# Two recurrence units per weight tile, and five Winograd pairs of gate tiles in place of three

## What is computed

```python
z = xn @ w_in
q, k, v, o, ig, fg, u, vb, ga, gb = split_in(z)
h, C, n, m = mlstm_branch(q, k, v, ig, lf, C, n, m)
y_a = (sigmoid(o) * h) @ w_a
y_b = spatial_gate(gelu(u), vn, w_s, b_s) @ w_b
x = x + (sigmoid(ga) * y_a + sigmoid(gb) * y_b) @ w_o
```

```python
# one chunk of one head
num = einsum('nhts,nhsv->nhtv', s, v) + w_inter[..., None] * einsum('nhvk,nhtk->nhtv', C, q)
h = num / maximum(abs(den), exp(-m_t))[..., None]
C_new = decay[..., None, None] * C + einsum('nhs,nhsv,nhsk->nhvk', w_last, v, k)
```

## Time and profile before

| what | us |
|---|---|
| median of 3 runs | 900.88 (900.83 to 901.25) |
| the profiled execution's own time | 900.66 |
| its span, first to last instruction | 898.8 |
| PE busy | 890.2 (99%) |
| DVE busy | 595.8 (66%) |
| ACT busy | 386.0 (43%) |
| POOL busy | 134.9 (15%) |
| mean granted TensorE clock | 0.998 |

### The profile page before, as it was taken

The page is one execution under the profiler, slowest core; times in us unless marked ns, Lnnn a source line. Parts: engine busy times, 40 slices in busy tenths (PEclk is TensorE's granted clock), DMA queues, the critical chain, the costliest instruction groups (busy, mean ns, idle before and its releaser), DMA issues.

```text
span 898.8 us, 19220 instructions
## 1 busy us (share of the span) xinstructions
PE 890.2 (99%) x7330; PEld 885.9 (99%) x7330; DVE 595.8 (66%) x946; ACT 386.0 (43%) x613; POOL 134.9 (15%) x182
## 2 busy tenths in 40 slices
PE   8999999999999999999999999999999999999997
PEld 8999999999999999999999999999999999999997
DVE  7895774443884445677755677777777778966544
ACT  7545434534863323344433344444444444433334
POOL 0673000002541111000005800000000000000001
PEclk9999999999999999999999999999999999999999
DMA  6332253234872222322355222222222222333232
GB/s 213 114 123 94 71 205 101 72 102 156 285 277 77 72 70 70 97 90 94 96 179 137 91 93 93 93 93 93 86 84 89 92 93 88 98 107 87 90 106 96
DMA packets 31495, 100.37 MB, mean 112 GB/s; under 512 B 4668, under 2 KB 7260, under 8 KB 31192
## 3 DMA queue, kind: packets, MB, share of 16 engines
q1 hardware_dynamic: 29256, 92.96, 31.5%
q0 software_dynamic: 1472, 5.72, 2.1%
q10 hardware_dynamic: 720, 1.04, 0.4%
HBM read 92.37 MB, written 7.35 MB: 111 GB/s over the span
## 4 chain that ended last, share of the span: by engine, by line
PE 91%; POOLq 3%; issue 3%; DMA 1%; POOL 1%; ACT 0%; SPq 0%; ACTq 0%
PE out L1924 84%; PE trp L1924 3%; PE aux L1924 2%; POOLq L1902 2%; POOLq L1900 1%; PE trp L1956 1%; DMA cwb<-in_conv_wb 1%; DMA raw_pair<-in_w_slots 1%; PE aux L2113 0%; POOL y L1915 0%; POOL out_conv_old L1886 0%; ACT xg L579 0%; POOLq L1893 0%; POOLq L87 0%; POOL sconv L1894 0%
## 5 line engine op out<-in xcount | busy, mean ns | idle before, releaser
L579 ACT ACTIVATE whi<-raw_pair 128x1024 fp32r<-128x1024 f32 (+3 forms) x164 | 154.5, 947 | 227.4 <-PE out L1924 213.6
L1068 DVE TENSOR_TENSOR wlo<-raw_pair,whi 128x1024 fp32r<-128x1024 f32 (+1 forms) x127 | 162.6, 1280 | 131.0 <-ACT whi L579 130.6
L1924 PE MATMUL out<-xh,whi 128*128 128x260 f32 x708 | 149.5, 288 | 0.0
L1924 PE MATMUL out<-xh,wlo 128*128 128x260 f32 x708 | 145.5, 283 | 0.0
L1924 PE MATMUL out<-xl,whi 128*128 128x260 f32 x708 | 145.4, 283 | 0.0
L1924 PE MATMUL out<-x2h,wlo 128*128 128x260 f32 x704 | 142.0, 283 | 0.0
L1924 PE MATMUL out<-x2h,whi 128*128 128x260 f32 x704 | 141.9, 283 | 0.0
L1924 PE MATMUL out<-x2l,whi 128*128 128x260 f32 x704 | 141.7, 283 | 0.0
L1924 PEld LDWEIGHTS out<-xh,whi 128*128 128x128 f32 x708 | 110.8, 189 | 0.5
L1924 PEld LDWEIGHTS out<-xh,wlo 128*128 128x128 f32 x708 | 110.3, 188 | 0.0
L1924 PEld LDWEIGHTS out<-xl,whi 128*128 128x128 f32 x708 | 110.2, 188 | 0.0
(11 more groups left out here) (362 smaller groups left out, 1683.0 us busy)
## 6 DMA issues: line engine op xcount, KB each, us to landing
raw_pair<-in_w_slots SPq DMA_DIRECT2D x123, 512.0 KB, 3.3
raw_pair<-in_w_dn SPq DMA_DIRECT2D x16, 448.0 KB, 3.3
c_ring<-in_C_state SPq DMA_DIRECT2D x8, 512.0 KB, 5.5
row<-scratch SPq DMA_DIRECT2D x8, 512.0 KB, 6.1
out_C_sample<-c_ring SPq DMA_DIRECT2D x8, 512.0 KB, 5.0
raw_pair<-in_w_dn SPq DMA_DIRECT2D x8, 512.0 KB, 3.5
xres<-in_x_all POOLq DMA_DIRECT2D x1, 1560.0 KB, 6.7
x<-in_x_all SPq DMA_DIRECT2D x5, 260.0 KB, 6.7
```

What stands on the lines that cost most here:

```text
L579: return act.activation(out, in_, func, **kw_)
L1068: TT(wlo[p][:, 0:width], raw[p][:, 0:width], whi[p][:, 0:width].bitcast(F32), ALU.subtract)\
L1924: return pe.matmul(*a, **k)
```

## The change

`WHOLE = NC + 2 = 6` BY pairs of tiles are plain, and five blocks follow: the first is of gate b (tiles 6 and 7, with the branch tiles of b), the other four of gate a (tiles 0 to 7). There are no plain AY steps any more. The number of slots and their order in memory stay.

The 16 units ride in the first 8 BY tiles, two in each: the products of unit 2m behind k-tile 0 and of unit 2m+1 behind k-tile 4; the transposes of unit 2m-1 behind k-tile 2 and of unit 2m behind k-tile 6. Tile 8 has the transposes of unit 15 behind k-tile 2. The loops over chunks are written out. All sums and differences of x now stand behind the last unit, beside BY tiles 8 to 11.

```diff
-PLAIN = 2
+WHOLE = NC + 2
 DOWN_PAIRS = 3
+GATE_PAIRS = KT - WHOLE // 2
...
-                self.n = [At(S_AY + 2 * PLAIN + 4 * q + t) for t in range(4)]
+                self.n = [At(S_BY + 2 * WHOLE + 4 * q + t) for t in range(4)]
+                self.of_b = q == 0
                 self.t0, self.t1 = self.n[0].c % 2, self.n[1].c % 2
-                self.j = PLAIN + 2 * q
+                self.j = WHOLE if self.of_b else 2 * q - 2
...
+            for m in range(2 * NC):
+                if m >= 1:
+                    split(At(S_BY + m + 1))
+                if m % 2 == 1:
+                    if m == 1:
+                        act.wait_ge(s_hal, 1)
+                    gate_sigmoid(At(S_BY + m - 1), m // 2 % 2)
+                unit_scaled(2 * m)
+                if m >= 1:
+                    unit_hi(2 * m - 1)
+                unit_scaled(2 * m + 1)
+                unit_hi(2 * m)
...
+            for m in range(2 * NC):
+                unit_denominator(2 * m)
+                if m >= 1:
+                    unit_gated(2 * m - 1)
+                    low(At(S_BY + m + 1))
+                if m % 2 == 0 and m >= 2:
+                    if m == 2:
+                        for r in range(4):
+                            dve.wait_ge(s_cs[r], 32)
+                    first_branch(At(S_BY + m - 1), m // 2 - 1, (m // 2 - 1) % 2)
+                if m >= 1:
+                    unit_low(2 * m - 1)
+                unit_denominator(2 * m + 1)
+                unit_gated(2 * m)
+                unit_low(2 * m)
...
+            def by_plain(i):
+                n = At(S_BY + 1 + 2 * i)
+                last = i == WHOLE - 1
+                if i == NC:
+                    unit_gated(NC * NH - 1)
+                    low(n)
+                    x_sum(0, 0, 0)
+                    first_branch(n.plus(-2), i - 1, (i - 1) % 2)
+                    unit_low(NC * NH - 1)
+                    x_sum(1, 0, 1)
+                    dve.drain()
+                    x_difference(0, 1, 0)
+                    x_sum(2, KT // 2, 1)
+                    dve.drain()
+                    x_difference(1, 2, 1)
+                    x_difference(2, 2, 0)
+                    low(n.plus(1))
+                    x_combination_low(0, 1)
                     x_sum(3, KT // 2, 0)
                     dve.drain()
                     x_difference(3, 3, 2)
-                    x_combination_low(2, 1)
+                    x_combination_low(2, 2)
                 if last:
                     x_combination_low(1, 3)
                     factor_low(pairs_w[0], 0)
                     factor_low(pairs_w[0], 1)
                     weight_sums(pairs_w[0])
...
+                first_branch(n, i, i % 2)
...
             def unit_transposes(c, t):
                 b = At(B_UNIT + t, c, 4)
+                pe.wait_ge(s_p, c * NH + t + 1)
...
+            def by_tile(m):
+
+                u = 2 * m
+                c, t = u // NH, u % NH
+                mids = {0: lambda: unit_products(c, t, c == 0), 4: lambda: unit_products(c, t + 1, c == 0),
+                        6: lambda: unit_transposes(c, t)}
+                if m >= 1:
+                    mids[2] = lambda: unit_transposes((u - 1) // NH, (u - 1) % NH)
+                tile(At(S_BY + m), *((xh, xl) if m % 2 == 0 else (hbh, hbl)), mids=mids)
```

More of the change, by code:

```diff
@@ L311, in hybrid_layer @@
         pairs_d = [DownPair(i) for i in range(DOWN_PAIRS)]
-        pairs_w = [Pair(q) for q in range((KT - PLAIN) // 2)]
+        pairs_w = [Pair(q) for q in range(GATE_PAIRS)]
         def vb_slot(j):
@@ L805, in _, with unit_scaled, unit_hi, gate_sigmoid @@
             A(hah[:, :, SEQ:TOK], so[:, :, SEQ:TOK]).then_inc(s_hah, 1)
[L808 to L823, removed]
+            def unit_scaled(u):
+                t = u % 2
+                act.wait_ge(s_rd, u + 1)
+                A(hn[t][:, :], trp[t][:, 0:2, :].rearrange("p a b -> p (a b)"), scale=nd[:, t, 2:3]).then_inc(tre[t], 1)
+            def unit_hi(u):
+                c, t = u // NH, u % NH
+                act.wait_ge(s_p, u + 2)
+                A(hah[:, 2 * t:2 * t + 2, c * P:(c + 1) * P], so[:, 2 * t:2 * t + 2, c * P:(c + 1) * P]).then_inc(s_hah, 1)
+            def gate_sigmoid(n, g):
+                ready(n)
+                A(both(ftmp[g][:, :]), out2(n), ACT.Sigmoid).then_inc(evac[n.c % 2], 1)
+            for m in range(2 * NC):
[10 more added lines that the diff above has]
+                unit_hi(2 * m)
             def merged_hi(j):
@@ L863, in ay_plain @@
                     split(n.plus(2))
[L864 to L866 removed]
+                gate_sigmoid(n, i % 2)
+                if i == NC:
+                    x_combination_hi(2)
                     x_combination_hi(1)
                 if last:
+                    x_combination_hi(3)
                     next_factors_hi(pairs_w[0])
@@ L907, in ay_pair @@
                     next_factors_hi(pairs_w[q + 1])
-                merged_hi(pr.j + 1)
-            for i in range(PLAIN):
-                ay_plain(i)
+                if not pr.of_b:
+                    merged_hi(pr.j + 1)
+            for i in range(NC, WHOLE):
+                by_plain(i)
             for pr in pairs_w:
@@ L1409, in unit_step @@
                 dve.reciprocal(nd[:, b, 2:3], nd[:, b, 1:2]).then_inc(s_rd, 1)
-                dve.wait_ge(s_unit, c * 4 + (t + 1))
+                dve.wait_ge(s_unit, u + 1)
                 STT(state[:, t, :], state[:, t, :], decay[:, c, t:t + 1], aux[:, 0, 0:DVA], ALU.mult, ALU.add)\
                     .then_inc(s_st, 1)
[L1413 to L1417, removed]
@@ new lines, in unit_low, with first_branch @@
+            def unit_low(u):
+                dve.wait_ge(s_hah, u + 2)
+                part = unit_part(u)
+                TT(hal[part], so[part], hah[part].bitcast(F32), ALU.subtract).then_inc(s_hal, 1)
+            def first_branch(n, j, g):
+                ready(n)
+                evacuated(dve, n.plus(-1))
+                TT(both(merged[:, j, :]), both(ftmp[g][:, :]), out2(n), ALU.mult).then_inc(evac[n.c % 2], 1)
+            for m in range(2 * NC):
[13 more added lines that the diff above has]
+                unit_low(2 * m)
@@ L1554, in ay_pair @@
                     first_gate_sum(pairs_w[q + 1])
-                merged_low(pr.j + 1)
-            for i in range(PLAIN):
-                ay_plain(i)
+                if not pr.of_b:
+                    merged_low(pr.j + 1)
+            for i in range(NC, WHOLE):
+                by_plain(i)
             for pr in pairs_w:
@@ L1924, in MM, with tile @@
                 return pe.matmul(*a, **k)
-            def tile(n, hi, lo, k0=0, nk=KT, bank=None, use=None, start=True, stop=True, mid=None, mid_at=3, each=None, end=None):
+            def tile(n, hi, lo, k0=0, nk=KT, bank=None, use=None, start=True, stop=True, mid=None, mid_at=3, each=None, end=None, mids=None):
                 p = n.c % 2
@@ L1943, in tile @@
                         mid()
+                    if mids is not None and k in mids:
+                        mids[k]()
                 m.then_inc(done, 1)
```

117 lines of the change are left out of this document (46 added, 71 removed).

## The result

| what | before | after |
|---|---|---|
| median, us (15 runs each) | 900.83 (900.57 to 901.53) | 902.76 (902.38 to 905.48) |
| the profiled execution's own time | 900.66 | 902.47 |
| its span | 898.8 | 900.1 |

The ratio is 1.0023, with a 95% interval of 1.0016 to 1.0030: slower by 1.93 us by the medians. The forecast was 902.8, with 1.9 us more.

The account below looks back on a forecast made before the run. The prediction took PE, busy 890.2 of 898.8 us, as the bound: waits of 2.0 + 0.1 + 1.9 + 0.9 = 4.9 us, less 2.99 for matmuls, give 1.9 us more, 902.8 us; range 900.5 to 904.9.

Parts of the forecast that it names:

- The matmuls: Two more gate pairs become blocks: 24 matmuls less on PE, 2.88 us, with 0.11 us of an old wait 2.99 less.
- The recurrence's steady state: BY tiles with two units: about 8.8 us each, DVE's 5.3 us of work fits, no wait, cost zero.
- The first BY tile: Unit 1's products behind k-tile 4 wait for unit 0's state update on DVE: 2.0 us, bounds 1.6 to 2.4.
- Behind the last unit: BY tiles 8 to 11: PE waits for DVE's queue, 0.1 us for a bank, 1.9 at tile 10, 0.9 at 11.
- T+2.65: T is the start of BY tile 8; DVE can start unit 15's gated product 2.65 us after it.
- T+13.64: The end of slot 10's low part on DVE, 13.64 us after the start of BY tile 8.
- The weights of the first block: Loaded into the buffer slot 11 frees, landing 3.3 us after issue; summed in time, half a microsecond to spare.
- the three signs: Signs of being wrong: second wait under 1 us, two-unit tile over 9 us, block of gate b waiting for weights.
- The drain rule: Full durations for DVE's operations, 0.07 us more each, would make the three waits about 3.5 us; the prediction used start spacings.
- rival 4: PE's clock falls to 1.2 GHz for one tile behind a wait: 5.8 us more, 908.6 us; chance 0.03.
- rival 1: The combinations hide in DVE's queue in BY tiles 8 and 9: 2.9 us of waits vanish, 899.9 us; chance 0.10.
- rival 2: Only the first BY tile's wait of 2.0 us is missing: 900.8 us; chance 0.09.

Follow-up runs that it names:

- e9: e5 with DVE's operations beside BY tiles 8 to 11 reordered so that none stands in front of ACT's result; 898.24 us.
- e6: The changed kernel with two more DVE additions of 128x1040, result unused, in each of five two-unit tiles; 902.64 us.
- e1: The changed kernel with unit 0's denominator and state update on DVE moved ahead of the last operations on the sample rows; 901.30 us.
- e2: The changed kernel with unit 1's products in the first BY tile moved from behind k-tile 4 to behind k-tile 7; 901.72 us.
- e11: The changed kernel with GpSimd's last product of the sample rows held until VectorE's updates of the step before are over; 905.37 us.
- e5: e4 with two sums of x moved into two of the recurrence's two-unit tiles; 899.02 us.
- e7: The changed kernel with one more DVE addition of 128x1040, result unused, ahead of the low part of slot 10; 903.91 us.
- e4: The changed kernel with the edits of e1 and e3 together; 899.16 us.
- e8: The changed kernel with four blocks, all of gate a, and eight plain BY pairs; 903.41 us.
- e3: The changed kernel with low parts of slots 10 and 11 ahead of differences and combinations' low parts, two of the latter moved into the block; 900.79 us.

## Why the prediction was right

**The matmuls.** Right. 24 are gone, and e9, without waits, has a stretch 3.08 us shorter than before (2.99 computed).

**The recurrence's steady state at zero.** Right, and safer than I had it. The first eight BY tiles take 69.79 us (263.34 to 333.13), 1.47 of them the wait, with no other gap, and BY tiles 2 to 7 last 8.74 to 8.79 us, where 8.8 was forecast. e6 shows 2.3 us of room per tile where I had argued with 0.7.

**The first BY tile, 2.0 us.** Right in mechanism (e1, e2, e11), too large by 0.5: 1.47. The step that failed is "nothing ahead of it on DVE has changed", which took 268.77 for a fixed start. The denominator began at 268.06. Of the 0.7 us, 0.59 is the group of eight updates: 3.29 us in the profiled execution of before, 2.70 in that of after, by the meeting with POOL. That is a difference of two executions, not of the two kernels: in e5 the same group took 3.79. The rest of the chain was as computed: the state update ended at 269.13, PE went on 0.14 later.

**Behind the last unit, 0.1 + 1.9 + 0.9.** Measured 0.06, 1.62 and 0.64. DVE's queue was computed well: T+2.65 was T+2.55, T+13.64 was T+13.43. The mis-sized term is the step from a low part's end to the tile that waited, 0.14 us from rows 9; here it is 0.05, twice. Each wait costs a little more than its gap, since the first matmuls behind it are slower: tile 10, whose first two take 0.51 us instead of 0.40, lasts 5.88 us without the gap at its end (346.61 to 353.13, less 0.64), where a plain tile lasts 5.76.

**The weights of the first block, "met, with half a microsecond to spare".** Wrong, and one of the three signs that the prediction itself named. The load was issued at 353.10 and the sums began at 357.71, 4.6 us later; I had taken the median of 3.3 us over the whole kernel (and 20.3 + 3.3 + 2.8 is 26.4, not 26.6). The block took 10.44 us, 0.36 more than the 10.08 of the others, where I had allowed none. This load took 4.3 to 4.7 us in each of the six kernels with this order, and the block 10.57 us in e1, 10.14 in e2, 10.21 in e6, 10.58 in e7 and 10.54 in e11. In the traces of e4 and e9, whose low parts come early, no such wait is seen.

**The drain rule.** DVE's starts were 1.13 to 1.15 us apart for operations of 1.22 to 1.24 (345.34, 346.48, 347.63; 351.86, 352.99, 354.14). With full durations the prediction had the waits 0.6 us longer, and they were shorter than forecast. The Trainium skill (VectorE: DVE Perf Modes, The DRAIN you can't avoid) says that the next operation does not start until the pipeline is empty, but the same section adds that an operation that is not held starts earlier, which the prediction left out. This trace agrees with the addition, for operations that do not read each other's result.

**The clock.** Waits of 1.3 and 1.5 us left the granted clock at 1.00 in both stages, the 2.4 GHz level, and matmuls at 0.12 us: rival 4 did not occur. It is 1.00 behind the longer waits of e7 (2.62 us) and e11 (2.76 us) too.

**The sum.** By e9, all waits cost 4.44 us instead of 4.9. So the stretch grew by 1.36 us, not 1.9. The profiled execution's own time grew by 1.81 and the median by 1.93. The rest lies in no stage: the span without the stretch is 696.1 us before and after (898.8 - 202.69 and 900.1 - 204.05). What grew is the time of an execution beyond its span, from the first to the last instruction: 1.9 us in the profiled execution of before, 2.4 in that of after. It is 1.80 to 1.91 us in each of 78 executions of the kernel before, 1.78 to 2.47 in those of the changed kernel (median 2.12), much the same in the other kernels with five blocks, and 1.81 to 1.90 in e8 with four. So it is not a chance of single executions. It goes with what e8 takes back, the fifth block, which is of gate b; why it does stays open. The two errors, 0.5 too much of waiting and some 0.5 of which no step spoke, cancelled: that the forecast was met to 0.04 us is luck; that PE waits for DVE at the three named places, and roughly how long, is not.

**Rivals 1 and 2.** They were a matter of order and not of capacity. e3 is rival 1 made by hand (899.9 forecast, 900.79 measured), and e1 is rival 2 (900.8 and 901.30); e9 is their common case, forecast as 897.9 and measured as 898.24.

## What to carry to other kernels

When work is taken off the bound engine and the helper engine's work is pushed together to make room, the average load does not say whether it fits. Add up the helper's queue by the spacing of its starts between the two events that fix it, and compare with the moment at which the bound engine needs each result. Operations that nobody awaits soon belong in front of a wait that exists anyway. Ahead of the low part for the next tile they may stand only as long as its input is not there: in e5 that low part stood first and DVE idled for 2.26 us, in e9 a sum and a difference fill this time, while in the changed kernel six of them made PE wait. e9 does the same work as the changed kernel in another order and is 4.5 us faster. A start time read from one execution is a sample; look for a releaser in brackets that is a DMA ahead of it, and keep its effect in the range.

## What the hardware showed unexpectedly

VectorE (DVE) and GpSimd (POOL) block each other. A VectorE update with two operands in SBUF (0.34 us alone) that started beside a GpSimd product over 128x1024 took 0.87, 1.46 and 1.95 us and ended 0.15 or 0.16 us behind it each time; with GpSimd held back the eight updates took 2.19 instead of 2.70 us. The Trainium skill (SBUF — State Buffer, SBUF: two separate sides) describes an exclusive lock on a port pair shared by the two engines, held for the whole instruction, and says that the loser fully blocks. The rows agree. It goes the other way too. In the changed kernel a GpSimd copy that takes 0.29 us alone takes 1.22 beside a low part on VectorE and ends 0.14 us behind it (timeline of DVE, then POOL):

```profile
260.27 1.22 DVE L1083 TENSOR_TENSOR wlo<-raw_pair,whi 128x1024 fp32r<-128x1024 f32 x1
260.41 1.22 POOL L1896 COPY sds<-sd 128x128 f32<-128x128 f32 x1 [2.05 <-DVE c_ring L1381]
...
262.18 0.29 POOL L1896 COPY sds<-sd 128x128 f32<-128x128 f32 x1
```

The stall stood in the trace of the kernel before, where it cost nothing; the change put VectorE's tail on the path and with it this wait for a load.
